# A 31-tap convolution shared by four engines: the shares, the place of the sums, and the last tiles by token halves

## The chip, the cores and the metric

The kernel runs on one core of a Trainium2 chip. The metric is the device time of one execution in microseconds (us). Before the change the median of three runs is 1353.84 us (1353.11 to 1364.42).

## The reference, cut to what matters

A program of two transformer-like blocks of two layers each, on 256 tokens of width 1024, all in fp32. The change is in one layer of the second block, the convolution layer. It is fed with a normalised `h` (256 tokens x 1024 features):

```python
def conformer_conv(h, w_pw1, b_pw1, w_dw, b_dw, ln_g, ln_b, w_pw2, b_pw2):
    a, gate = jnp.split(h @ w_pw1 + b_pw1, 2, axis=-1)
    u = a * jax.nn.sigmoid(gate)
    dw = lax.conv_general_dilated(           # each feature by itself, 31 taps back in time
        u, w_dw[:, None, :], window_strides=(1,), padding=((CONV_WIDTH_2 - 1, 0),),
        dimension_numbers=('NWC', 'WIO', 'NWC'), feature_group_count=D_MODEL) + b_dw
    d32 = dw.astype(jnp.float32)
    mu = jnp.mean(d32, axis=-1, keepdims=True)
    var = jnp.mean(jnp.square(d32 - mu), axis=-1, keepdims=True)
    z = (d32 - mu) * lax.rsqrt(var + EPS) * ln_g + ln_b
    z = jax.nn.silu(z).astype(h.dtype)
    return z @ w_pw2 + b_pw2
```

The mean and the variance go over all 1024 features of a token, so no token can be normalised before the last feature tile of that token is summed.

## The kernel before, in words

Every engine runs its own program (`pe_program` TensorE, `act_program` ScalarE, `dve_program` VectorE, `pool_program` GpSimd, `sp_program` the DMA queue). The order in each is written by hand. They meet only at named semaphore values (`sig`, `at`).

**Weights.** 200 chunks of up to 1 MB (`PLAN`) come through one DMA queue into three buffers `raw`. For each chunk ScalarE writes a rounded copy `whi` (`hi(n)`), VectorE the rest `wlo = raw - whi` (`lo(n)`), and TensorE multiplies in three passes, high x high, high x low, low x high (`mm3`). `hi(n)` waits until TensorE has done chunk n-3, and the DMA of chunk n until `lo(n-3)` is done.

**The convolution layer** has features on the partitions and tokens along the free axis: eight feature tiles of 128 x 256. `stationary` makes two 128 x 256 products of `w_pw1` from one chunk with 48 matmuls; eight chunks in all. Before the change a chunk holds two tiles of `a` or two of the gate, so tiles are ready in pairs, after each second chunk. ScalarE makes the sigmoid, VectorE `u` (a tile of `up`, signal `up{ft}`). The 31 taps of a tile are shared out: tap 0 with the bias is ScalarE's (`tap0`), the last `ON_PE[ft]` taps are matmuls with a diagonal matrix that holds the 128 weights of the tap (line 953), and the rest are VectorE's multiply-adds over 128 x 256 (line 1489) into `cv` in SBUF. ScalarE makes the diagonals too, one by one, in a ring of 12 (`diagonals`). VectorE adds TensorE's sum from PSUM (`add_taps`). GpSimd has no part in the taps.

**The norm** needs `cv` turned to tokens: `stats_of(t, c)` turns four tiles of token half t (line 405), VectorE takes the statistics (lines 2085, 2124), GpSimd the power -1/2 (lines 2243, 2171), VectorE normalises 128 x 512 pieces (line 1486), TensorE turns them back, ScalarE applies `silu` and rounds (`cz`, `chi`), VectorE makes the low part (`clo`). The output product with `w_pw2` (`rows_out`, 24 matmuls of 512 columns a chunk, 4 chunks) takes two feature tiles a chunk for all tokens at once, so it begins when the norm of both token halves is done.

The layers around it are SwiGLU layers (`ffn_stage`), bound by TensorE; the one before is number 2.

## Time and profile before

| What | Value |
|---|---|
| median of three runs | 1353.84 us |
| the profiled execution | 1352.12 us |
| its span in the trace | 1350.3 us |
| TensorE, VectorE, ScalarE, GpSimd busy | 96%, 68%, 53%, 4% of the span |
| mean granted TensorE clock | 0.989 |
| convolution layer, first matmul of `w_pw1` to the last of the taps | 1027.6 to 1120.3 us |
| from there to the first matmul of `w_pw2` | 1120.3 to 1129.8 us |
| from there to the turning of the next layer's input | 1129.8 to 1152.9 us |

The execution lasts 1.8 us longer than its span, for what lies around it. Times in the rows are microseconds from the span's start. A TensorE row's duration has latency in it that overlaps the next one, so matmuls are costed by the distance of their starts. The same holds for VectorE and ScalarE, to a smaller part.

### The profile page before, as it was taken

The page shows a single profiled execution, that of the slowest core. Times are in us where ns is not written, and L with a number is a line of the kernel's source. Part 1 is how long each engine was busy: PE and PEld are TensorE (multiplying, and loading weights), DVE is VectorE, ACT ScalarE, POOL GpSimd, SP SyncE. Part 2 cuts the span into 40 slices and gives each one's busy share as a digit, 9 for nine tenths or more (in the row PEclk, how much of TensorE's full clock was granted, in tenths as well). Part 3 has the DMA queues.
Part 4 walks back from the last instruction along what each step waited for, and adds up shares of the span by engine and source line. Part 5 has one row for each costly group of instructions (what it writes and reads, how often), then busy time and mean ns, then how long its engine had stood idle before and what let it go on. Part 6 is the DMA issues. An engine that isn't in the chain of part 4 may idle for free.

```text
span 1350.3 us, 17591 instructions
## 1 busy us (share of the span) xinstructions
PE 1291.1 (96%) x7034; PEld 1105.2 (82%) x7034; DVE 918.5 (68%) x1274; ACT 713.0 (53%) x1074; POOL 54.8 (4%) x80
## 2 busy tenths in 40 slices
PE   5999999999999878999999999999998998999997
PEld 5998778888888667888888877888888996888886
DVE  4967565766666676666667856766666896776665
ACT  5765444654445654554445544544446664554443
POOL 0000000100001400100000001000000000100000
PEclk9999999999999989999999999999999998999999
DMA  6453235455554411455555633555554321455551
GB/s 243 157 184 128 94 111 201 156 197 188 191 188 147 155 59 55 142 210 187 187 188 180 221 138 137 182 189 189 191 189 158 110 78 63 156 187 187 203 189 60
DMA packets 30785, 215.17 MB, mean 159 GB/s; under 512 B 3552, under 2 KB 3808, under 8 KB 5488
## 3 DMA queue, kind: packets, MB, share of 16 engines
q1 hardware_dynamic: 30704, 214.05, 45.0%
q8 instruction: 56, 0.92, 0.3%
q14 instruction: 25, 0.20, 0.0%
HBM read 212.99 MB, written 1.05 MB: 159 GB/s over the span
## 4 chain that ended last, share of the span: by engine, by line
PE 88%; DVE 5%; ACT 4%; POOL 1%; issue 1%; DMA 0%; SPq 0%; POOLq 0%; ACTq 0%; DVEq 0%
PE pb L428 23%; PE pb L399 15%; PE pb L401 14%; PE pb L400 14%; PE pb L430 11%; PE pb L953 3%; PE pb L405 2%; DVE wlo L1476 2%; ACT both L1020 1%; ACT whi L1016 1%; ACT arena L1020 1%; DVE arena L1480 1%; POOL st L2171 1%; PE pb L793 1%; DVE both L1489 1%
## 5 line engine op out<-in xcount | busy, mean ns | idle before, releaser
L1476 DVE TENSOR_TENSOR wlo<-raw,whi 128x2048 fp32r<-128x2048 f32 (+3 forms) x205 | 456.9, 2230 | 225.4 <-ACT whi L1016 225.2
L428 PE MATMUL pb<-both,whi 128*128 128x512 f32 x1344 | 477.0, 399 | 0.0
L1016 ACT ACTIVATE whi<-raw 128x2048 fp32r<-128x2048 f32 (+2 forms) x201 | 380.4, 1896 | 84.1 <-PE pb L401 81.6
L430 PE MATMUL pb<-both,wlo 128*128 128x256 f32 x1344 | 377.3, 281 | 0.0
L399 PE MATMUL pb<-whi,both 128*128 128x512 f32 (+1 forms) x754 | 298.2, 396 | 10.5 <-DVE both L1489 4.5
L428 PEld LDWEIGHTS pb<-both,whi 128*128 128x128 f32 x1344 | 252.5, 188 | 62.4
L401 PE MATMUL pb<-whi,both 128*128 128x512 f32 (+1 forms) x754 | 293.7, 390 | 0.0
L400 PE MATMUL pb<-wlo,both 128*128 128x512 f32 (+1 forms) x754 | 293.3, 389 | 0.0
L430 PEld LDWEIGHTS pb<-both,wlo 128*128 128x128 f32 x1344 | 253.8, 189 | 1.5
L1020 ACT ACTIVATE arena<-pb 128x256 f32<-128x256 f32 (+1 forms) x248 | 102.8, 427 | 259.7 <-PE pb L430 164.6
L399 PEld LDWEIGHTS pb<-whi,both 128*128 128x128 f32 x754 | 142.4, 189 | 43.1 <-issue 6.7
L401 PEld LDWEIGHTS pb<-whi,both 128*128 128x128 f32 x754 | 142.3, 189 | 30.8
L400 PEld LDWEIGHTS pb<-wlo,both 128*128 128x128 f32 x754 | 142.6, 189 | 26.7
L1480 DVE TENSOR_TENSOR arena<-arena 128x512 f32<-128x512 f32 (+3 forms) x187 | 122.1, 658 | 14.8 <-ACT arena L1020 3.8
L1480 DVE TENSOR_TENSOR arena<-arena,pb 128x256 f32<-128x256 f32 (+1 forms) x189 | 75.4, 423 | 53.2 <-ACT arena L1020 48.8
L399 PE MATMUL pb<-both,whi 128*128 128x256 f32 (+1 forms) x296 | 86.2, 291 | 3.5 <-DVE wlo L1476 2.4
L400 PE MATMUL pb<-both,whi 128*128 128x256 f32 (+1 forms) x296 | 84.4, 285 | 0.0
L401 PE MATMUL pb<-both,wlo 128*128 128x256 f32 (+1 forms) x296 | 84.3, 285 | 0.0
L1020 ACT ACTIVATE arena<-arena 128x512 f32<-128x512 f32 (+5 forms) x75 | 47.1, 632 | 68.4 <-DVE arena L1480 60.7
L1489 DVE SCALAR_TENSOR_TENSOR arena<-arena,cols 128x256 f32<-128x256 f32 x170 | 70.6, 480 | 6.0 <-ACT arena L1020 5.2
L405 PE MATMUL pb<-c,arena 128*128 128x128 f32 (+1 forms) x286 | 43.1, 296 | 22.1 <-ACT arena L1020 14.3
L1020 ACT ACTIVATE both<-arena 128x256 fp32r<-128x256 f32 x96 | 35.4, 412 | 52.8 <-DVE arena L1480 52.5
(121 smaller groups left out, 989.0 us busy)
## 6 DMA issues: line engine op xcount, KB each, us to landing
raw<-d_ws SPq DMA_DIRECT2D x196, 1024.0 KB, 4.9
raw<-d_ws SPq DMA_DIRECT2D x3, 768.0 KB, 4.3
arena<-d_c SPq DMA_DIRECT2D x1, 1060.0 KB, 4.9
xt<-d_x SPq DMA_DIRECT2D x2, 512.0 KB, 4.1
arena<-d_rows SPq DMA_DIRECT2D x2, 512.0 KB, 5.0
out<-arena SPq DMA_DIRECT2D x2, 512.0 KB, 2.6
raw<-d_ws SPq DMA_DIRECT2D x1, 640.0 KB, 3.8
c<-d_c SPq DMA_DIRECT2D x1, 385.0 KB, 5.0
```

Source lines behind the costliest of these rows:

```text
L399: e.matmul(out, lh, rh, start=start, stop=False)
L400: e.matmul(out, lh, rl, start=False, stop=False)
L401: return e.matmul(out, ll, rh, start=False, stop=stop)
L405: return e.transpose(out, a, ident[0:k, 0:k])
L428: e.matmul(b[:, :], wh[:, k, fs], both[:, k, :], start=k == 0, stop=k == 7, skip_group_check=True)
L430: m = e.matmul(b[:, 256:512], wl[:, k, fs], ahi[:, k, :], start=False, stop=k == 7, skip_group_check=True)
L953: m = e.matmul(b[:, 0:256], T.diag[:, tap[0] % NG, :], T.up[:, ft, w:w + 256], start=w == 31 - ON_PE[ft], stop=w == 30)
L1016: e.activation(whi[:, n % NH, 0:width(n)], raw[:, n % NR, 0:width(n)], ACT.Copy).then_inc(*sig("act.hi", f"hi{n}"))
L1020: e.activation(out, a, func, **kw).then_inc(*sig(key, *([name] if name else [])))
L1476: e.tensor_tensor(wlo[:, n % NH, a:b], raw[:, n % NR, a:b], f32(whi[:, n % NH, a:b]), ALU.subtract).then_inc(*sig("dve.lo", f"lo{n}"))
L1480: e.tensor_tensor(out, a, b, op).then_inc(*sig(key, *names))
L1489: e.scalar_tensor_tensor(out=out, in0=a, scalar=s, in1=b, op0=op0, op1=op1).then_inc(*sig(key, *names))
```

## The change

- **Shares of the taps.** TensorE has 79 taps in place of 106 (7, 8, 8, 8, 8, 9, 13, 18 by tile), VectorE 106 in place of 134, GpSimd sums 55 (7 or 8 a tile, 3 in the last). ScalarE makes GpSimd's products (`products`), in a ring of 12; the first one of a tile starts the sum `part`. GpSimd adds the others, 47 additions, and then `part` onto `cv` (`join`), once more a tile.
- **VectorE's sums lie in PSUM** (`acc`, banks 5 to 7). The last tap writes `cv` in SBUF. It works on two tiles in turn: the rest of one and the first `FIRST` taps of the next.
- **The diagonals are loaded**, 5 MB in five DMAs during SwiGLU layer 2, in place of being made by ScalarE.
- **Gates beside features.** The columns of `w_pw1` are interleaved, so that each chunk gives one tile's `a` and its gate, and a tile is ready with every chunk.
- **The last tiles, the norm and the output by token halves.** TensorE's taps of tiles 6 and 7 are done for tokens 0 to 127 first, and the norm of these goes on while the taps of the others are multiplied. `out_part` makes the first two chunks of the output for one token half at a time. GpSimd's sum of tile 7 goes in by a matmul with the identity.
- In all four SwiGLU layers ScalarE's last `hi` stands ahead of a wait for VectorE, not behind it.

```diff
 
-ON_PE = (12, 12, 12, 12, 12, 12, 17, 17)
-NG = 12
+ON_PE = (7, 8, 8, 8, 8, 9, 13, 18)
+ON_POOL = (7, 8, 7, 8, 7, 8, 7, 3)
+ON_DVE = tuple(30 - a - b for a, b in zip(ON_PE, ON_POOL))
+FIRST = (10, 7, 7, 7, 7, 7, 6, 15)
+DIAG0 = tuple(sum(ON_PE[:i]) for i in range(8))
+NX = 12
+AHEAD = 1
...
         self.mv = room(4)
-        self.diag = room(128 * NG, NG)
+        self.part = room(256 * 3, 3)
+        self.prod = room(256 * NX, NX)
...
                     sp_load(e, "pos", ret.pi, d_pos)
+                for i in range(len(DIAG_LOADS)):
+                    if n == CHUNK["gate2", 3 + i]:
+                        if i == 0:
+                            e.wait_ge(*at("x5.11"))
...
+                def taps(ft, name, spot, tokens, mid=None, then=None):
+
+                    b = claim(name, spot)
                     e.wait_ge(*at(f"up{ft}"))
...
-                    b = claim(f"ln{t}{c}")
+                    for i in range(ON_PE[ft]):
+                        n, w = DIAG0[ft] + i, 31 - ON_PE[ft] + i
+                        if i == mid:
+                            then()
+                        if i == 0 or n % 16 == 0:
+                            e.wait_ge(*at(f"in.diag{n // 16}"))
+                        m = e.matmul(b[:, 0:tokens.stop - tokens.start], T.diag[:, n, :],
+                                     T.up[:, ft, w + tokens.start:w + tokens.stop], start=i == 0, stop=w == 30 and ft < 7)
+                    if ft < 7:
+                        m.then_inc(*sig(key, f"{name}.m"))
+                    else:
+                        e.wait_ge(*at("sum7"))
+                        m = e.matmul(b[:, 0:128], ident, T.part[:, 1, tokens], start=False, stop=True)
+                        m.then_inc(*sig(key, f"{name}.m"))
...
+                for p in range(8):
+                    stationary(key, CHUNK["pw1", p], claim(f"p1.{p}", p % 3), f"p1m{p}", 6 if p == 0 else None)
+                    if 1 <= p <= 6:
+                        taps(p - 1, f"tp{p - 1}", 3 + (p - 1) % 2, slice(0, 256))
+                for ft in (5, 6, 7):
+                    ring.take(f"acc{ft}", 5 + ft % 3)
+                taps(6, "tp6.0", 3, slice(0, 128))
+                stats_of(0, 0, 2)
+                stats_of(1, 0, 0)
+                taps(7, "tp7.0", 1, slice(0, 128))
+                taps(6, "tp6.1", 7, slice(128, 256), 8, lambda: stats_of(0, 1, 5))
+                taps(7, "tp7.1", 4, slice(128, 256), 10, lambda: turn(0, 0, 3))
+                turn(0, 1, 2)
+                stats_of(1, 1, 7)
+                b0 = [claim(f"out6.0{c}", 4 + c) for c in range(2)]
+                out_part(0, 0, b0)
+                out_part(0, 1, b0, lambda: turn(1, 0, 1))
+                turn(1, 1, 0)
+                b1 = [claim(f"out6.1{c}", 6 + c) for c in range(2)]
+                out_part(1, 0, b1)
+                out_part(1, 1, b1)
+                for j in (2, 3):
...
                         e.wait_ge(*at(f"f{f}.h{j}"))
                         if j >= 2:
                             e.wait_ge(*at(f"done{CHUNK[f'down{f}', j - 2]}"))
                         for i in range(2):
                             run(key, f"f{f}.hhi{j}.{i}", ahi[:, 8 + (2 * j + i) % 4, :],
                                 ffn.hh[:, j % 2, 256 * i:256 * i + 256], ACT.Copy)
-                    if j == 10:
-                        hi(CHUNK[f"down{f}", 9] + 2)
                 if f > 1:
                     hi(CHUNK[f"down{f}", 10] + 2)
                     for c in range(2):
...
+                def products(ft, a, b):
+
+                    for i in range(a, min(b, ON_POOL[ft])):
+                        w = 1 + ON_DVE[ft] + i
+                        if i == 0:
...
+                        if made[0] >= NX:
+                            e.wait_ge(*at(f"summed{made[0] - NX}"))
+                        run(key, f"prod{made[0]}", T.prod[:, made[0] % NX, :], T.up[:, ft, w:w + 256], ACT.Copy,
+                            scale=col("w_dw", 8 * w + ft))
+                        made[0] += 1
+
+                def gate(ft):
+                    e.wait_ge(*at(f"p1m{ft}"))
+                    if ft >= 2:
+                        e.wait_ge(*at(f"up{ft - 2}"))
+                    run(key, f"sg{ft}", T.sg[:, ft % 2, :], bank(f"p1.{ft}")[:, 256:512], ACT.Sigmoid,
+                        bias=col("b_pw1", 8 + ft))
+
+                def first_tap(ft):
+                    e.wait_ge(*at(f"up{ft}"))
+                    e.wait_ge(*at(f"acc{ft - 3}.gone" if ft >= 3 else "sq6.11"))
+                    run(key, f"tap0.{ft}", bank(f"acc{ft}")[:, 0:256], T.up[:, ft, 0:256], ACT.Identity,
+                        scale=col("w_dw", ft), bias=col("b_dw", ft))
+
+                for p in range(8):
+                    if p:
+                        gate(p - 1)
+                    hi(CHUNK["pw1", p] + 2)
+                    if p:
+                        first_tap(p - 1)
+                        products(p - 1, 0, 4)
+                        if p == 7:
+                            gate(7)
+                        products(p - 1, 4, 31)
+                first_tap(7)
+                products(7, 0, 31)
+                run(key, None, T.sg[:, 0, 0:1], T.sg[:, 0, 0:1], ACT.Silu)
+                hi(CHUNK["pw2", 2])
...
+                def tap(ft, w, a=0, b=256):
+
+                    name, end = f"dwt{ft}" + (f".{a // 128}" if ft == 7 else ""), w == ON_DVE[ft]
+                    acc = bank(f"acc{ft}")[:, a:b]
+                    e.wait_ge(*at(f"tap0.{ft}" if w == 1 else name))
+                    stt(key, [name] + ([f"acc{ft}.gone"] if end and b == 256 else []), T.cv[:, ft, a:b] if end else acc,
+                        T.up[:, ft, w + a:w + b], col("w_dw", 8 * w + ft), acc, ALU.mult, ALU.add)
+
+                def taps(p, a, b):
+
+                    for i in range(a, b):
+                        w = 1 + FIRST[p - 1] + i
+                        if p and w <= ON_DVE[p - 1]:
+                            tap(p - 1, w)
+                        if i < min(FIRST[p], ON_DVE[p]):
+                            tap(p, 1 + i, 0, 128 if p == 7 else 256)
+
+                def gated(ft):
+                    e.wait_ge(*at(f"sg{ft}"))
+                    stt(key, [f"up{ft}", f"p1.{ft}.gone"], T.up[:, ft, 30:286], bank(f"p1.{ft}")[:, 0:256], col("b_pw1", ft),
+                        T.sg[:, ft % 2, :], ALU.add, ALU.mult)
+
+                def add_taps(ft, name, a=0, b=256):
+                    e.wait_ge(*at(f"{name}.m"))
+                    e.wait_ge(*at(f"dwt{ft}" + (f".{a // 128}" if ft == 7 else "")))
+                    tt(key, [("dx" if ON_POOL[ft] and ft < 7 else "dw") + name[2:], f"{name}.gone"], T.cv[:, ft, a:b], T.cv[:, ft, a:b],
+                       bank(name)[:, 0:b - a], ALU.add)
...
+                for p in range(8):
+                    if p:
+                        gated(p - 1)
+                        taps(p - 1, 0, AHEAD)
+                    lo(CHUNK["pw1", p] + 2)
+                    if p:
+                        taps(p - 1, AHEAD, 2 if p == 7 else 30)
+                    if p == 7:
+                        gated(7)
+                        taps(6, 2, 30)
+                    if p >= 2:
+                        add_taps(p - 2, f"tp{p - 2}")
+                taps(7, 0, 30)
+                add_taps(6, "tp6.0", 0, 128)
+                add_taps(7, "tp7.0", 0, 128)
+                stats_of(0, 0)
+                stats_of(1, 0)
+                for w in range(1, 2):
+                    tap(7, w, 128, 256)
+                stats_of(0, 1)
+                aggregate(0)
+                for w in range(2, 5):
+                    tap(7, w, 128, 256)
+                normal(0, 0)
+                normal(0, 1)
+                for w in range(5, ON_DVE[7] + 1):
...
             rstd_x("pool.conf", 6)
+            made = 0
+
+            def join(ft, name, a, b):
+
+                e.wait_ge(*at(f"dx{name}"))
+                tt("pool.conf", [f"dw{name}", f"part.gone{ft}"], conf.cv[:, ft, a:b], conf.cv[:, ft, a:b],
+                   conf.part[:, ft % 3, a:b], ALU.add)
+
+            for ft in range(8):
+                acc = conf.part[:, ft % 3, :]
+                for i in range(1, ON_POOL[ft]):
+                    if i == 1:
+                        e.wait_ge(*at(f"part{ft}"))
+                    else:
+                        own()
+                    e.wait_ge(*at(f"prod{made}"))
+                    tt("pool.conf", [f"summed{made}", f"sum{ft}"], acc, acc, conf.prod[:, made % NX, :], ALU.add)
+                    made += 1
+                if ft and ft < 7 and ON_POOL[ft - 1]:
+                    own()
+                    join(ft - 1, f"{ft - 1}", 0, 256)
             for t in range(2):
+                own()
+                join(6, f"6.{t}", 128 * t, 128 * t + 128)
```

On **TensorE**, behind the last `stationary` product of the kernel before, line 953 is a tap (two instructions in the trace) and line 405 a transpose:

```order
L953 MATMUL pb<-arena 128x256 x12
L405 MATMUL pb<-c,arena 128x128 x8
L953 MATMUL pb<-arena 128x256 x34
L405 MATMUL pb<-c,arena 128x128 x16
L399 MATMUL pb<-whi,both 128x512
```

The same place in the changed kernel, where line 971 is a tap, 977 the identity matmul, 417 a transpose and 411 the first output matmul:

```order
L971 MATMUL pb<-arena 128x128 x13
L417 MATMUL pb<-c,arena 128x128 x8
L971 MATMUL pb<-arena 128x128 x18
L977 MATMUL pb<-arena,c 128x128
L971 MATMUL pb<-arena 128x128 x8
L417 MATMUL pb<-c,arena 128x128 x4
L971 MATMUL pb<-arena 128x128 x15
L417 MATMUL pb<-c,arena 128x128 x4
L971 MATMUL pb<-arena 128x128 x8
L977 MATMUL pb<-arena,c 128x128
L417 MATMUL pb<-c,arena 128x128 x8
L411 MATMUL pb<-whi,both 128x512
```

The 12 and 34 taps of 256 tokens are now 13 and 18 for each half, and statistics and turned pieces of the first half stand between taps of the second.

On **VectorE**, one pair of tiles of the kernel before (line 1476 is `lo`, 1489 makes `u` or a tap, 1480 adds TensorE's sum):

```order
L1476 TENSOR_TENSOR wlo<-raw,whi 128x2048
L1480 TENSOR_TENSOR arena<-arena,pb 128x256 x2
L1489 SCALAR_TENSOR_TENSOR arena<-arena,cols 128x256 x22
L1476 TENSOR_TENSOR wlo<-raw,whi 128x2048
L1489 SCALAR_TENSOR_TENSOR arena<-pb,cols,arena 128x256 x2
L1489 SCALAR_TENSOR_TENSOR arena<-arena,cols 128x256 x14
```

One tile of the changed kernel (1542 makes `u` or a tap, 1529 is `lo`, 1533 adds):

```order
L1542 SCALAR_TENSOR_TENSOR arena<-pb,cols,arena 128x256
L1542 SCALAR_TENSOR_TENSOR pb<-arena,cols,pb 128x256 x2
L1529 TENSOR_TENSOR wlo<-raw,whi 128x2048
L1542 SCALAR_TENSOR_TENSOR pb<-arena,cols,pb 128x256 x12
L1542 SCALAR_TENSOR_TENSOR arena<-arena,cols,pb 128x256
L1533 TENSOR_TENSOR arena<-arena,pb 128x256
```

The taps read one tensor from SBUF and the sum from PSUM, where both lay in SBUF; each tile makes its round with one chunk.

On **GpSimd**, behind the power of the layer's first norm, nothing stood but the powers of the second one. Now:

```order
L2242 TENSOR_TENSOR arena<-arena 128x256 x53
L2242 TENSOR_TENSOR arena<-arena 128x128
L2337 TENSOR_SCALAR arena<-arena 128x1
L2242 TENSOR_TENSOR arena<-arena,c 128x1
L2242 TENSOR_TENSOR arena<-arena 128x128
```

The powers (2337 and 2242 on 128x1) stand behind 47 additions of products and six whole and one half `join`.

## Rows read from the trace of the kernel before

**Rows 1.** The page: busy time, share of the span, instructions of each engine.
```profile
PE 1291.1 (96%) x7034; PEld 1105.2 (82%) x7034; DVE 918.5 (68%) x1274; ACT 713.0 (53%) x1074; POOL 54.8 (4%) x80
PE 88%; DVE 5%; ACT 4%; POOL 1%; issue 1%; DMA 0%; SPq 0%; POOLq 0%; ACTq 0%; DVEq 0%
```

**Rows 2.** Stretches: length, busy time and count of each engine, clock, DMA.
```profile
1027.60:1120.30 92.70, 92.70 (x604) 86.97 (x605) 80.63 (x166) 60.19 (x137) 0.00 (x0) 1.00 0.26 92
1120.30:1129.80 9.50, 3.40 (x19) 2.50 (x17) 5.58 (x10) 1.56 (x4) 1.59 (x4) 0.81 0.00 1
1129.80:1153.30 23.50, 23.50 (x103) 19.34 (x104) 13.75 (x15) 12.61 (x20) 0.00 (x0) 0.93 0.34 115
```

**Rows 3.** The chain of waits in the layer: start, us, what.
```profile
1045.25 5.18 PE pb L953 x24
...
1056.19 5.18 PE pb L953 x24
...
1105.97 14.70 PE pb L953 x68
1120.69 0.43 DVE arena L1480
...
1129.79 0.77 PE pb L399
...
1130.98 0.43 PE pb L401
...
1133.58 0.23 PE pb L399
...
1152.93 0.45 PE pb L405 x4
```

**Rows 4.** Timeline of TensorE: start, us, line, operation, shape, count.
```profile
129.20 1.95 PE L601 MATMUL pb<-arena 128*128 128x128 f32 x16
...
1104.93 1.04 PE L405 MATMUL pb<-c,arena 128*128 128x128 f32 x8
```

**Rows 5.** Timeline of VectorE.
```profile
48.75 2.97 DVE L1489 SCALAR_TENSOR_TENSOR arena<-arena,cols 128x256 f32<-128x256 f32 x6 [0.32 <-ACT arena L1020]
...
94.17 1.12 DVE L1486 TENSOR_SCALAR arena<-pb,arena 128x128 f32<-128x128 f32 x4
...
1050.08 2.29 DVE L1476 TENSOR_TENSOR wlo<-raw,whi 128x2048 fp32r<-128x2048 f32 x1
1052.28 5.62 DVE L1489 SCALAR_TENSOR_TENSOR arena<-arena,cols 128x256 f32<-128x256 f32 x14
...
1108.72 10.38 DVE L1489 SCALAR_TENSOR_TENSOR arena<-arena,cols 128x256 f32<-128x256 f32 x26
```

**Rows 6.** Groups by shape, 1010 to 1170 us: busy us, mean ns, idle before.
```profile
L1480 DVE TENSOR_TENSOR arena<-arena,pb 128x256 f32<-128x256 f32 x12 | 4.6, 415 | 1.3 <-PE pb L953 1.3
...
L1020 ACT ACTIVATE arena<-arena,cols 128x256 f32<-128x256 f32 x8 | 4.4, 593 | 4.3 <-DVE arena L1489 4.3
...
L1480 DVE TENSOR_TENSOR both<-arena,both 128x256 fp32r<-128x256 f32 x10 | 4.2, 425 | 8.8 <-ACT both L1020 8.8
```

**Rows 7.** Timelines of VectorE and GpSimd around one `lo`.
```profile
1161.37 2.29 DVE L1476 TENSOR_TENSOR wlo<-raw,whi 128x2048 fp32r<-128x2048 f32 x1 [0.21 <-ACT whi L1016]
...
1161.45 2.62 POOL L2171 TENSOR_TENSOR st<-st,c 128x1 f32<-128x1 f32 x1
...
1164.53 0.55 POOL L2171 TENSOR_TENSOR st<-st,c 128x1 f32<-128x1 f32 x1
```

**Rows 8.** GpSimd's line 2171: min, median, max ns; six 128x32, six 128x512.
```profile
L2171 POOL TENSOR_TENSOR arena<-arena x12: 249/1290/3397, 448.5 to 473.4; 128x32 f32<-128x32 f32 x6, 128x512 f32<-128x512 f32 x6
```

**Rows 9.** SwiGLU layer 2: waits (total us, times, longest) and the stretch.
```profile
ACT whi L1016 <- PE pb L401: 15.0, 8, 1.9
...
860.00:1015.00 155.00, 155.00 (x811) 131.94 (x810) 102.65 (x116) 76.83 (x94) 0.00 (x0) 1.00 0.54 190
```

**Rows 10.** Timeline of VectorE at the end of SwiGLU layer 2.
```profile
1014.75 4.49 DVE L1476 TENSOR_TENSOR wlo<-raw,whi 128x2048 fp32r<-128x2048 f32 x2 [1.35 <-ACT whi L1016]
```

More of the change, by code:

```diff
@@ L93 @@
 STAGES = ("ssd", "ffn0", "mla", "ffn1", "ret", "ffn2", "conf", "ffn3", "end")
-LOADS = ("x0", "x1", "c0", "cols", "w2", "c1", "c2", "pw", "pos", "rows", "fg")
+DIAG_LOADS = tuple(f"diag{i}" for i in range(5))
+LOADS = DIAG_LOADS + ("x0", "x1", "c0", "cols", "w2", "c1", "c2", "pw", "pos", "rows", "fg")
 class Tally:
@@ L989, in conf_stage, with turn @@
-                ring.over = (0, 1, 2, 3)
-                turn(0)
-                for j in range(4):
-                    if j < 3:
-                        turn(j + 1)
-                    rows_out(key, 6, CHUNK["pw2", j], bs, (2 * j, 2 * j + 1), (f"clo{2 * j}", f"clo{2 * j + 1}"),
-                             j == 0, j == 3, (lambda: turn_half("pe.ffn3", 7, 0)) if j == 3 else None)
+                def turn(t, c, spot):
+                    b = claim(f"ct{t}{c}", spot)
+                    e.wait_ge(*at(f"dn{t}{c}"))
+                    for i in range(4):
+                        m = tr(b[:, 128 * i:128 * i + 128], T.dn[:, t, 512 * c + 128 * i:512 * c + 128 * i + 128])
+                    m.then_inc(*sig(key, f"ctm{t}{c}"))
@@ new lines, in out_part @@
+                def out_part(t, j, bs, mid=None):
+                    wh, wl = weights(CHUNK["pw2", j])
+                    for c in range(2):
+                        if mid and c:
+                            mid()
+                        for k in range(2):
+                            e.wait_ge(*at(f"clo{2 * j + k}.{t}"))
+                            m = mm3(bs[c][:, :], ahi[:, 2 * j + k, 128 * t:128 * t + 128],
+                                    alo[:, 2 * j + k, 128 * t:128 * t + 128], wh[:, k, half(c)], wl[:, k, half(c)],
+                                    j == 0 and k == 0, False)
+                    m.then_inc(*sig(key, *([f"done{CHUNK['pw2', j]}"] if t else [])))
@@ L1439, in turn @@
-                def turn(j):
-                    e.wait_ge(*at(f"ctm{j}"))
-                    for i in range(2):
-                        ft = 2 * j + i
-                        run(key, f"cz{ft}", T.cv[:, ft, :], bank(f"ct{j}")[:, 256 * i:256 * i + 256], ACT.Silu,
-                            scale=col("ln_g", ft), bias=col("ln_b", ft))
-                        own()
-                        run(key, f"chi{ft}", ahi[:, ft, :], T.cv[:, ft, :], ACT.Copy)
-                    tally.value[f"ct{j}.gone"] = at(f"cz{2 * j + 1}")
+                made = [0]
@@ L1449, in conf_stage @@
                 turn(0)
-                for j in range(3):
-                    turn(j + 1)
-                    hi(CHUNK["pw2", j] + 2)
+                turn(1)
+                hi(CHUNK["pw2", 3])
+                hi(CHUNK["pw2", 3] + 1)
             ssd_stage()
@@ L2121, in conf_stage, with aggregate @@
[L2121 to L2122 removed]
+                def aggregate(t):
                     own()
                     e.bn_aggr(T.mv[:, 2 * t:2 * t + 2], T.bst[:, 12 * t:12 * t + 12]).then_inc(*sig(key, f"cmv{t}"))
[L2125 to L2129 removed]
@@ new lines, in conf_stage @@
+                add_taps(6, "tp6.1", 128, 256)
+                add_taps(7, "tp7.1", 128, 256)
+                losses(0, range(0, 2))
+                stats_of(1, 1)
+                aggregate(1)
+                losses(0, range(2, 4))
+                normal(1, 0)
+                losses(0, range(4, 8))
+                normal(1, 1)
+                losses(1, range(3))
+                lo(CHUNK["pw2", 2])
+                losses(1, range(3, 8))
+                e.wait_ge(*at("in.rows"))
+                for t in range(2):
+                    tt(key, [], xt[:, t, :], xt[:, t, :], T.rows, ALU.add)
```

178 lines of the change are left out of this document (51 added, 127 removed).

## The prediction

> **What bounds the kernel now.** First the page: TensorE is busy for 96% of the span and holds 88% of the chain that ended last [rows 1]. The reader should see that a saving elsewhere is worth nothing unless TensorE waits for it. Then the stretches of the convolution layer [rows 2]: from 1027.6 to 1120.3 TensorE is busy for all of 92.7 us; from 1120.3 to 1129.8 it does 3.4 us of work and the granted clock is 0.81; then it is busy again, but at 0.93. The chain of waits [rows 3] gives the parts:
> - 12 taps start at 1045.25, last 5.18 and come again at 1056.19, so the 48 matmuls of a chunk take 10.94 - 5.18 = 5.76 us, and a tap 5.18/12 = 0.432. The last 34 taps say the same: 14.70/34 = 0.432. The stretch is 8 x 5.76 + 106 x 0.432 + 0.9 for eight transposes = 92.8 us. It is TensorE's own work and nothing else.
> - Then the norm stands open, 9.5 us from the last tap to the first output matmul (1129.79).
> - Behind it an output matmul takes 0.43 us, from 1133.1 on 0.23: after the pause TensorE is at the lower level of its clock, 1.2 GHz, then at 2.4. 90 output matmuls lie between 1129.79 and 1152.93, with 0.9 for eight transposes. At 0.2275 each that would be 21.4 us; it took 23.1, so the low clock costs 1.8.
>
> So the layer lasts 1152.93 - 1027.6 = 125.3 us. VectorE is busy for 80.6 of the first 92.7 us and ScalarE for 60.2 [rows 2]; these two are what limits how much can be moved off TensorE.
>
> **The change, part by part.**
>
> *TensorE.* Tiles 0 to 5 have 48 taps: 20.8 us. Tiles 6 and 7 have 31, each in two halves of 128 tokens. No tap of 128 tokens is in the trace; the nearest is line 601, eight products of 128x128 in 16 instructions that take (1.95 - 0.28)/15 = 0.112 each [rows 4] (0.28 is what one lasts), so 0.223 a product. Two halves cost 0.446 against 0.432 for a whole tap, and 62 halves 13.8 us; splitting costs 0.4 us in all. With eight chunks (46.1), two identity matmuls (0.4), 32 transposes, 0.45 for four [rows 3] (3.6), and 90 output matmuls (20.5) TensorE's own work to the same point is 105.2 us, against 114.0 before (125.3 less the 9.5 and the 1.8). The diagonals' making is off ScalarE; on TensorE that saves nothing.
>
> *VectorE.* A tap costs 10.38/26 = 0.40 where two tiles are taken in turn, and 0.50 where each waits for the one before ((2.97 - 0.48)/5) [rows 5]. Each tile's round is `lo` 2.20 (1050.08 to 1052.28), `u` 0.40, 13 or 14 taps 5.4, TensorE's sum 0.37: 8.4 us. I add 0.3 for the wait between `u` and the first tap of the tile, since ScalarE makes tap 0 in PSUM in between (0.59 at most [rows 6], against one other tap that covers 0.40), and 0.4 for GpSimd (below): 9.1. TensorE's round is 5.76 + 8 x 0.432 = 9.2. So they run almost even. Followed tile by tile from the first `u` at 1034.4, VectorE is through the first half of tile 7 at about 1104.5 (7 `lo` 15.4, 8 `u` 3.2, 97 taps 38.8 and 0.9 for the nine that stand alone, 9 half taps at (1.12 - 0.29)/3 = 0.28 [rows 5], in turn with others, 2.7, sums 2.8, waits for first taps 3.4, GpSimd 2.8). TensorE is there at 1027.6 + 46.1 + 20.8 + 13 x 0.223 + 0.9 + 19 x 0.223 = 1102.5. TensorE does 8 taps of the second half meanwhile (1.8 us) and then waits some 1 us for the last sums of the first.
>
> *The taps' sums in PSUM.* No VectorE row writes PSUM. An addition with an operand in PSUM takes 415 ns, one with all in SBUF 425 [rows 6], so I take the same 0.40. The bounds are 0.40 and 0.50, the distance at which taps follow each other singly. The Trainium skill (VectorE: DVE Perf Modes, The TRN2 errata) gives VectorE a fixed 120 cycles with a PSUM source against 58 from SBUF, which would add 0.065 us a tap, or 6.9 over 106, if it held; the two rows here don't show it. As a result of its own it is the first rival.
>
> *GpSimd.* Its additions of 32 and 512 elements take 0.249 and 1.290 us (least and median [rows 8]; the six of each shape stand below and above). On the line between them 256 elements take 0.74; with 0.08 for the wait between two, 0.81. Up to the sum of tile 7 it has 47 additions and six joins: 43 us. While VectorE runs a `lo`, it stands: an operation of 0.55 us took 2.62 when it was issued 0.08 after the start of one [rows 7]. Seven `lo` lie in its way: 7 x 2.2 = 15.4. So its round is 7.7 x 0.81 + 2.2 = 8.4, under 9.2, and from the first product at about 1037 it needs to 1095.8; as each tile's sum begins only with ScalarE's first product, I see it at 1102, just in time for tile 7. Ends: 0.25 and 1.29 an addition. The same row is why a `lo` may also wait for GpSimd, up to 0.74. The Trainium skill (SBUF, Who interferes with whom) calls it an exclusive lock of a pair of ports that VectorE takes with two inputs in SBUF; by that rule a tap with its sum in PSUM does not take it, and the row agrees for `lo`. No row here shows a tap beside GpSimd, in either form.
>
> *ScalarE.* Its round is `hi` 1.9, gate, tap 0 and 7 or 8 products at 0.59 or less [rows 6]: 7.5, hidden under 9.2. `hi` stands ahead of the products, so a late GpSimd does not hold the weights back until the ring of 12 is full.
>
> *The diagonals' loads.* 5 x 1 MB during SwiGLU layer 2, where the DMA engines are busy for 0.54 of the time and TensorE is never idle [rows 9]. ScalarE's `hi` waits there for TensorE alone, never for data, so the chunks come early. A chunk's 5.6 us of matmuls hold 3.0 us of transfer and 2.6 free; a load of 3.0 comes with every third chunk, into 7.8 free: 0. If the cover were gone, 5 x 3 = 15 us.
>
> *Norm and output.* The last half sums of tokens 0 to 127 are turned at about 1105.5. Statistics 0.65, aggregate 0.25, GpSimd 0.9 and two pieces of 0.7 take 3.5 to 4.2 us; TensorE has 15 half taps (3.3), and then turns the pieces and does 8 more (1.8). Second half: its last sum at about 1112.0, a `join` of 0.5, transposes to 1112.9. The output of the first token half begins there, 24 matmuls or 5.5 us, and the second norm (4 us) is inside it. The second half's 24 and the last 48 follow without a gap; both `lo` for them end 1 to 2 us early. The turning of the next input, at 1152.93 before, comes at 1112.9 + 0.9 + 90 x 0.2275 = 1134.3. The waits in this are about 1 us at the sums of the first half and 0.4 at the second join, so 105.2 + 1.4 = 106.6 from 1027.6 on, the same place. The 1.8 us of low clock go too, as no pause is over 1.5 us.
>
> *The moved `hi`.* At the end of SwiGLU layer 2, VectorE's two `lo` start at 1014.75 and end at 1019.2, after `hi` [rows 10]; with the first 1.4 us earlier the second starts 0.4 earlier, as it waits for TensorE. Gain 0.4 there, 0 in the other three, whose end is set by TensorE.
>
> **The sum.** 1152.93 - 1134.3 = 18.6, and 0.4: 19.0 us less. The profiled execution of 1352.1 would be 1333.1; the median of the runs is 1.7 higher, and gives 1334.8. Forecast 1335 us, 0.986 of before.
>
> **The rivals.**
> 1. *VectorE becomes the bound, since a sum in PSUM costs more.* At 0.50 a tap its round is 10.5 against 9.2. VectorE already ends 2 us behind TensorE, so some 97 x 0.1 = 9.7 us go onto the path: 1344.5. For it: VectorE was at 87% of this stretch. Against it: the 415 and 425 ns.
> 2. *GpSimd becomes the bound.* At 1.0 an addition with its wait, in place of 0.81, 53 x 0.19 = 10 us; 2 to 3 hide in its slack, 1343. For it: its round has only 0.8 to spare, and each `lo` blocks it. It would show as TensorE or VectorE waiting for line 2242.
> 3. *Taps and GpSimd's additions exclude each other*, as `lo` and GpSimd do [rows 7], even with the sum in PSUM. Then the 70 us of VectorE and the 43 of GpSimd come one after the other, and the first half is complete at 1034.4 + 113 = 1147 in place of 1105: 1335 + 42 = 1377, slower. It decides from the point where more than 19 of the 43 us are not beside the taps. The same ending has a smaller form: half of them blocked, 1356.
> 4. *The norm is not covered*: the second half's taps run out, TensorE pauses twice for 2 us more and comes back at the low clock, as in [rows 3], for 1.8: 1341.
>
> **How the numbers follow.** Forecast 0.67 (1331 to 1339), rivals 1 and 2 0.11 and 0.08, rival 3 0.05, rival 4 0.09. Lowest: no waits and no GpSimd delay, 2 us less, with TensorE alone setting the pace from 1331 on, and 1 for spread: 1330. The range 1330 to 1345 leaves out rival 3 and the upper parts of 1 and 2. About 1% (13.5 us) is what a measurement of this kernel can tell from no change. Faster by over 1%, under 1340.3: the forecast and a third of the others' chance, 0.75; within 1% 0.20; slower 0.05.
>
> **What would show it.** TensorE busy without a gap up to about 1094; tap pitch 0.432 and half tap 0.223; taps of VectorE at 0.40 with `pb` as output; GpSimd's 128x256 at 0.74, and longer only beside `lo`; first output matmul near 1113 in place of 1129.8, at 0.23. The forecast is wrong if a VectorE tap takes 0.5, if GpSimd's rows grow beside taps, or if TensorE waits for the weights in any chunk.

## The result, and the profile after

The changed kernel takes 1331.4 us (median of 4 runs, 1330.8 to 1333.6) against 1356.3 for the kernel before (4 runs, 1353.1 to 1364.4, the three of the forecast and one more): a ratio of 0.984, 95% interval 0.980 to 0.987. Forecast were 1335, range 1330 to 1345. The profiled execution took 1331.6, its span 1329.8. In the lines below `pb` is PSUM and `arena` SBUF.

The page, which answers to [rows 1]:

```profile
PE 1278.7 (96%) x7046; PEld 1098.0 (83%) x7046; DVE 911.4 (69%) x1265; ACT 704.0 (53%) x1040; POOL 105.7 (8%) x135
...
PE 89%; DVE 4%; ACT 4%; POOL 1%; issue 1%; DMA 0%; SPq 0%; POOLq 0%; ACTq 0%; DVEq 0%
```

TensorE is as busy as before; its stream is 12.4 us shorter, and GpSimd has 51 us of new work. The layer in stretches, against [rows 2]; behind the length stand the busy time and count of TensorE, its weight loads, VectorE, ScalarE and GpSimd, then the granted clock, the DMA share and GB/s:

```profile
1025.20:1094.00 68.80, 68.80 (x483) 66.26 (x484) 59.52 (x111) 44.01 (x77) 45.65 (x47) 0.97 0.33 115
1094.00:1104.20 10.20, 10.20 (x93) 10.09 (x93) 9.60 (x27) 6.56 (x11) 4.81 (x7) 1.00 0.15 63
1104.20:1111.30 7.10, 7.08 (x62) 6.72 (x61) 6.58 (x18) 2.70 (x10) 1.25 (x3) 1.00 0.00 1
1111.30:1132.70 21.40, 21.40 (x100) 17.64 (x100) 15.74 (x25) 11.79 (x30) 0.92 (x2) 1.00 0.41 145
```

The reader should see the second number beside the first in each row: TensorE is busy for all of the layer, and the stretch of 9.5 us with 3.4 of work is gone. The chain of waits, against [rows 3]:

```profile
1084.24 3.89 PE pb L971 x18
...
1093.88 2.90 PE pb L971 x26
...
1104.21 3.35 PE pb L971 x30
1107.58 0.63 PE pb L417 x4
...
1111.26 0.27 PE pb L411
...
1113.62 0.23 PE pb L412
...
1132.68 0.45 PE pb L417 x4
```

Nine taps of 256 tokens (18 instructions) take 3.89, 0.432 each; 13 of 128 take 2.90, 0.223 each. The first output matmul starts at 1111.26, 18.5 us sooner than before, and runs at 0.23 from the start. The next input is turned at 1132.68, 20.25 us sooner.

Where the 20.25 come from, by places that both traces have: 17.8 in the layer (from its first matmul at 1025.19 to 1132.68 are 107.5 us, 125.3 before), 0.5 in SwiGLU layer 2 ahead of it, and 1.9 earlier, of which 1.5 lie in the first layer, where no instruction was changed: from 19 to 26 us the granted clock was 0.76 in the trace before and 1.00 in this one. That part differs from one execution to the next and is not the change's.

The other engines, timelines of VectorE and, in the second fence, of GpSimd around one `lo`, against [rows 5] and [rows 7]:

```profile
1060.52 0.48 DVE L1542 SCALAR_TENSOR_TENSOR pb<-arena,cols,pb 128x256 f32<-128x256 f32 x1
1061.24 0.49 DVE L1542 SCALAR_TENSOR_TENSOR pb<-arena,cols,pb 128x256 f32<-128x256 f32 x1 [0.24 <-ACT pb L1055]
1061.64 2.28 DVE L1529 TENSOR_TENSOR wlo<-raw,whi 128x2048 fp32r<-128x2048 f32 x1
1063.84 4.79 DVE L1542 SCALAR_TENSOR_TENSOR pb<-arena,cols,pb 128x256 f32<-128x256 f32 x12
```
```profile
1060.35 0.75 POOL L2242 TENSOR_TENSOR arena<-arena 128x256 f32<-128x256 f32 x1 [0.53 <-DVE arena L1533]
1062.18 7.19 POOL L2242 TENSOR_TENSOR arena<-arena 128x256 f32<-128x256 f32 x7 [1.08 <-ACT arena L1055]
```

Twelve taps with their sum in PSUM take 4.79, so 0.40 each, while GpSimd adds beside them: seven additions from 1062.18 to 1069.37, through a `lo`. An addition alone lasts 0.74. VectorE was even ahead at the last chunk, where it stood for 2.29 us until the next tile's gate was there:

```profile
1094.42 0.48 DVE L1542 SCALAR_TENSOR_TENSOR arena<-pb,cols,arena 128x256 f32<-128x256 f32 x1 [2.29 <-ACT arena L1055]
```

The groups from 1005 to 1150, against [rows 6, 8] (busy us, mean ns, idle before):

```profile
L2242 POOL TENSOR_TENSOR arena<-arena 128x256 f32<-128x256 f32 x53 | 50.0, 944 | 28.9 <-ACT arena L1055 22.9 <-DVE arena L1533 2.9
...
L1542 DVE SCALAR_TENSOR_TENSOR pb<-arena,cols,pb 128x256 f32<-128x256 f32 x90 | 38.8, 485 | 3.5 <-ACT pb L1055 3.2
...
L1529 DVE TENSOR_TENSOR wlo<-raw,whi 128x2048 fp32r<-128x2048 f32 x16 | 36.5, 2288 | 7.1 <-ACT whi L1051 7.1
...
L1055 ACT ACTIVATE arena<-arena,cols 128x256 f32<-128x256 f32 x55 | 22.9, 496 | 0.0
```

GpSimd's 53 additions would be 39.2 us at 0.74; the 10.8 above that I put down to time under a `lo`, in which the additions stand. The `lo` itself lasts 2.29, as before.

### The profile page after: what moved, and what is told of

It reads as the page before. It is cut to its first block, busy times and chain, and to the rows that moved or that the text cites. A ratio compares the mean times of both kernels' runs of the same rounds, so it can differ in the third digit from the quotient of the medians.

```text
span 1329.8 us, 17700 instructions
## 1 busy us (share of the span) xinstructions
PE 1278.7 (96%) x7046; PEld 1098.0 (83%) x7046; DVE 911.4 (69%) x1265; ACT 704.0 (53%) x1040; POOL 105.7 (8%) x135
## 4 chain that ended last, share of the span: by engine, by line
PE 89%; DVE 4%; ACT 4%; POOL 1%; issue 1%; DMA 0%; SPq 0%; POOLq 0%; ACTq 0%; DVEq 0%
PE pb L440 23%; PE pb L411 15%; PE pb L413 15%; PE pb L412 15%; PE pb L442 12%; PE pb L971 3%; PE pb L417 2%; DVE wlo L1529 1%; ACT both L1055 1%; ACT whi L1051 1%; ACT arena L1055 1%; POOL st L2242 1%; PE pb L805 1%; DVE arena L1533 1%; DVE both L1542 1%
## 5 line engine op out<-in xcount | busy, mean ns | idle before, releaser
L1533 DVE TENSOR_TENSOR arena<-arena,pb 128x256 f32<-128x256 f32 (+2 forms) x191 | 75.9, 421 | 51.7 <-ACT arena L1055 48.1
L2250 POOL TENSOR_SCALAR st<-st 128x1 f32<-128x1 f32 (+2 forms) x26 | 9.4, 363 | 1111.9 <-DVE st L1533 917.8
L1055 ACT ACTIVATE arena<-arena 128x512 f32<-128x512 f32 (+6 forms) x76 | 47.3, 626 | 68.4 <-DVE arena L1533 60.8
L2242 POOL TENSOR_TENSOR arena<-arena 128x256 f32<-128x256 f32 (+3 forms) x67 | 65.5, 982 | 46.9 <-ACT arena L1055 22.9
L1055 ACT ACTIVATE both<-arena 128x256 fp32r<-128x256 f32 (+1 forms) x104 | 37.0, 396 | 47.1 <-DVE arena L1533 47.1
```

What stands on the lines that cost most here:

```text
L1055: e.activation(out, a, func, **kw).then_inc(*sig(key, *([name] if name else [])))
L1533: e.tensor_tensor(out, a, b, op).then_inc(*sig(key, *names))
L2242: e.tensor_tensor(out, a, b, op).then_inc(*sig(key, *names))
```

## The experiments

Each is the changed kernel with one edit. Whole times of one kernel scatter by up to 14 us (its granted clock between 0.981 and 0.994), so the layer's own length is read beside them: from its first matmul to the turning of the next input. A repeat of the changed kernel gives the measure for that.

> The changed kernel unaltered, beside the others of this set, as their reference. Expected 1331 us, and 107.0 to 107.5 us from the layer's first matmul to the turning of the next input. In the first profile 1.8 of the 107.5 lay in the first chunk of the layer, at a granted clock of 0.96. If that comes from what the change does there, it comes again; if it is the throttle's own doing, it may be gone, and the layer takes 105.7.

1334.5 us, ratio 0.987 [0.983, 0.991], and **105.85 us** for the layer (1030.94 to 1136.79). The granted clock around the layer's first matmul, in the first profile (it starts at 1025.19) and in this one (1030.94):

```profile
1023.00:1029.00 6.00, 5.44 (x26) 5.04 (x25) 3.98 (x9) 5.59 (x10) 0.00 (x0) 0.50 0.39 156
```
```profile
1023.40:1026.40 3.00, 0.00 (x0) 0.00 (x0) 2.17 (x7) 2.59 (x9) 1.21 (x3) 0.96 0.19 49
1027.00:1029.00 2.00, 2.00 (x11) 2.00 (x10) 0.49 (x1) 0.72 (x1) 0.03 (x1) 0.50 0.97 330
1029.90:1034.00 4.10, 3.20 (x27) 3.06 (x26) 3.23 (x9) 4.08 (x9) 0.00 (x0) 1.00 0.12 50
```

In both, TensorE stands for 3.4 us at a clock that is still high, and turns the layer's input for the most part at the low one (0.50, the level of 1.2 GHz). What differs is how long the low stretch lasts: about 3.4 us here, over before the first matmul, and 6.8 us in the first profile, to 1029.1. There it covers the first part of the layer's first chunk too, which takes 7.5 us from its first matmul to the next chunk's in place of 5.9. Of the eleven profiles with the change or parts of it two have the long stretch. The instructions are the same in both, and why it is long in some executions is not known. So 105.8 is the layer without it, and the measure below.

**1. The sums back in SBUF.** VectorE's running sums and ScalarE's tap 0 use `cv` in place of the PSUM bank.

```diff
-                    acc = bank(f"acc{ft}")[:, a:b]
+                    acc = T.cv[:, ft, a:b]
...
-                    run(key, f"tap0.{ft}", bank(f"acc{ft}")[:, 0:256], T.up[:, ft, 0:256], ACT.Identity,
+                    run(key, f"tap0.{ft}", T.cv[:, ft, :], T.up[:, ft, 0:256], ACT.Identity,
```

> VectorE's sums lie in SBUF again, all else as in the changed kernel. Theory 1, that place matters because VectorE and GpSimd exclude each other whenever VectorE reads two tensors in SBUF: GpSimd's 53 additions (43 us) no longer fit beside 106 taps, GpSimd's round grows from 8.2 us to about 14 us in place of 9.2, its 128x256 rows last 1 us and more in the mean over 0.944, and the kernel takes 25 to 45 us more than the changed one, 1355 to 1375 us. Theory 2, only the long subtractions exclude GpSimd and a tap of 0.4 us slips in between: within 3 us of 1331.4.

1353.6 us, ratio to before 1.000 [0.999, 1.002]; the layer takes 126.0. The whole gain hangs on this one edit. Its timeline of VectorE, of GpSimd, its groups, and what TensorE waited for (total, times, longest):

```profile
1060.32 7.75 DVE L1542 SCALAR_TENSOR_TENSOR arena<-arena,cols 128x256 f32<-128x256 f32 x12
```
```profile
1058.62 6.79 POOL L2242 TENSOR_TENSOR arena<-arena 128x256 f32<-128x256 f32 x6 [1.10 <-ACT arena L1055]
```
```profile
L1542 DVE SCALAR_TENSOR_TENSOR arena<-arena,cols 128x256 f32<-128x256 f32 x97 | 63.8, 711 | 2.4 <-ACT arena L1055 2.1
...
L2242 POOL TENSOR_TENSOR arena<-arena 128x256 f32<-128x256 f32 x53 | 52.9, 999 | 43.8 <-ACT arena L1055 23.0 <-DVE arena L1533 17.7
...
L971 PE MATMUL pb<-arena 128*128 128x256 f32 x96 | 25.4, 424 | 7.4 <-DVE arena L1542 7.4
```
```profile
PE pb L971 <- DVE arena L1542: 10.1, 6, 2.3
PE pb L977 <- POOL arena L2242: 3.3, 1, 3.3
PE pb L417 <- POOL arena L2242: 1.7, 1, 1.7
```

Twelve taps take 7.75 in place of 4.79. A tap rises from 485 to 711 ns in the mean, 21.9 us over 97, while an addition of GpSimd rises from 944 to 999 only, 2.9 us over 53: it is VectorE that loses, 0.47 us for each of the 47 additions ahead of the last sum. The round of a tile goes from 9.0 to 12.1 us in the mean of six, and TensorE stands for 15.1 us, two thirds of it for line 1542. The granted clock, 0.96 from 1034 to 1080 and 0.95 from there to 1112, takes 3.4 more. My expectation had the loser wrong, GpSimd, and 1353.6 lies just below its 1355 to 1375.

The means hide how clean the split is. Single instructions, an addition with the tap beside it, a tap with no addition beside it, and an addition that met a `lo` (1058.11 to 1060.39):

```profile
1061.07 0.81 POOL L2242 TENSOR_TENSOR arena<-arena 128x256 f32<-128x256 f32 x1
```
```profile
1061.19 0.97 DVE L1542 SCALAR_TENSOR_TENSOR arena<-arena,cols 128x256 f32<-128x256 f32 x1
...
1067.59 0.47 DVE L1542 SCALAR_TENSOR_TENSOR arena<-arena,cols 128x256 f32<-128x256 f32 x1
```
```profile
1058.62 2.37 POOL L2242 TENSOR_TENSOR arena<-arena 128x256 f32<-128x256 f32 x1 [1.10 <-ACT arena L1055]
```

Of the 97 taps 50 lie beside an addition and last 0.83 to 0.97 us; 45 have none beside them and last 0.47 to 0.49, with a product of ScalarE beside them (10) or without; two meet only the edge of one. So ScalarE's products are not the cause. A tap and an addition together take 0.88 from one pair to the next, where additions in the changed kernel follow each other every 0.81: VectorE goes at GpSimd's pace. In these pairs the addition starts ahead of the tap, mostly by 0.13 us, and under a `lo` it starts behind it. In both it is the one that starts second that stands.

**2. The same without GpSimd's additions.** Sums in SBUF as in run 1, and the 45 additions of tiles 0 to 6 with their products left out (the output lacks those taps). One product a tile and the joins stay, a join waits for that product, and VectorE's and TensorE's shares stay as they are.

```diff
-ON_POOL = (7, 8, 7, 8, 7, 8, 7, 3)
-ON_DVE = tuple(30 - a - b for a, b in zip(ON_PE, ON_POOL))
+ON_DVE = tuple(30 - a - b for a, b in zip(ON_PE, (7, 8, 7, 8, 7, 8, 7, 3)))
+ON_POOL = (1, 1, 1, 1, 1, 1, 1, 3)
```

> VectorE's sums in SBUF as in the run with the sums in SBUF, and GpSimd's additions of 128x256 left out but for tile 7: 38 or so products and their additions are not computed, so the output lacks those taps; VectorE, TensorE and the joins are as in the changed kernel. Theory (with sums in SBUF a tap and an addition of GpSimd exclude each other, and nothing else is slow about SBUF): the taps are back at 0.40, VectorE's round at 9 us or less, the layer lasts 105 to 107 us as in the changed kernel. Rival (a tap with its sum in SBUF is slow by itself): the round stays at 11.5 and the layer at 126.

```profile
L1542 DVE SCALAR_TENSOR_TENSOR arena<-arena,cols 128x256 f32<-128x256 f32 x97 | 43.3, 501 | 2.4 <-ACT arena L1055 2.1
```
```profile
1056.19 4.83 DVE L1542 SCALAR_TENSOR_TENSOR arena<-arena,cols 128x256 f32<-128x256 f32 x12
```
```profile
1070.99 0.74 POOL L2242 TENSOR_TENSOR arena<-arena 128x256 f32<-128x256 f32 x1 [8.73 <-DVE arena L1533]
```
```profile
1071.13 0.88 DVE L1542 SCALAR_TENSOR_TENSOR arena<-arena,cols 128x256 f32<-128x256 f32 x1
```

Timeline and groups show the taps back at 0.40, and the layer at 107.4 (1027.77 to 1135.15), 1334.0 us in the one run. So the place of the sum is free by itself and costs only beside an addition of GpSimd. The last two rows show the rest: where one of the remaining joins lies beside a tap, that tap takes 0.88 again. Five taps do so, and one beside tile 7's additions takes 0.95. These six cost VectorE 2.5 us, and the 1.6 us of the layer over 105.8 are mostly a wait of TensorE of 1.4 us for the first half's last sum.

**3. The norm behind the taps.** The statistics of the first half stand behind all of the second half's taps.

```diff
-                taps(6, "tp6.1", 7, slice(128, 256), 8, lambda: stats_of(0, 1, 5))
-                taps(7, "tp7.1", 4, slice(128, 256), 10, lambda: turn(0, 0, 3))
+                taps(6, "tp6.1", 7, slice(128, 256))
+                taps(7, "tp7.1", 4, slice(128, 256))
+                stats_of(0, 1, 5)
+                turn(0, 0, 3)
```

> TensorE turns the sums and the normalised pieces of the first token half only after all taps of the second. Theory 1, the cover by taps is what removed most of the old pause: the chain of turning, statistics, power and normalising (about 3.9 us, from 1103.7 to 1107.6) and the turning back stand open, the first output matmul comes 4 to 6 us later, with some 1 us of low clock, so 1336 to 1338. Theory 2, the split output alone does it, since its second half has work anyway: under 1.5 us more.

1341.3 us, ratio 0.990 [0.985, 0.995]; the layer takes 113.2 (1031.68 to 1144.89), 7.4 over 105.8. Its chain and its window:

```profile
1113.84 0.45 PE pb L417 x4
1114.31 0.71 DVE arena L2158
...
1119.86 0.69 PE pb L417 x2
```
```profile
1112.00:1136.00 24.00, 19.65 (x93) 15.77 (x92) 16.08 (x38) 11.66 (x34) 2.28 (x5) 0.86 0.09 31
```

TensorE stands for 4.35 us in this window, at whose granted clock of 0.86 another 3.4 of the 24 us are lost. Covering the norm by half taps is worth 7.4 us of the gain. That is more than my expectation, which had 1 us for the clock; rival 4 had priced the loss at 6.

**4. Two more taps a tile on TensorE**, taken from GpSimd (14 in all, the two of tile 6 in halves, tile 7 as it was; a sixth load brings the diagonals).

```diff
-ON_PE = (7, 8, 8, 8, 8, 9, 13, 18)
-ON_POOL = (7, 8, 7, 8, 7, 8, 7, 3)
+ON_PE = (9, 10, 10, 10, 10, 11, 15, 18)
+ON_POOL = (5, 6, 5, 6, 5, 6, 5, 3)
```

> Two taps more on TensorE and two less on GpSimd in each of tiles 0 to 6; 93 diagonals, six loads. Theory 1, TensorE sets the pace of the whole layer: 12 x 0.432 for tiles 0 to 5 and 2 x 0.446 for tile 6 make 6.1 us more, 1337.5. Theory 2, VectorE or GpSimd set it: 0 to 3 us more, as GpSimd's relief pays for part.

1339.6 us, ratio 0.989 [0.986, 0.993]; the layer takes 111.45, 5.6 more. Twelve whole taps and four half ones are 12 x 0.432 + 4 x 0.223 = 6.1: the work added is paid nearly in full, so TensorE sets the pace of the changed kernel. The 0.5 are small waits that it had, spread over the transposes and half taps behind 1100: the distances there are longer in the repeat of the changed kernel (1.01 against 0.84 us for the last eight transposes ahead of the output) and count as busy time.

**5. The other way: six, three, and six with another order on GpSimd.** Taps of tiles 0 to 5 go from TensorE to VectorE, one a tile or in tiles 0, 2 and 4 only. In the third kernel GpSimd adds tile 7's products before it joins tile 5.

```diff
-ON_PE = (7, 8, 8, 8, 8, 9, 13, 18)
+ON_PE = (6, 7, 7, 7, 7, 8, 13, 18)
```
```diff
-ON_PE = (7, 8, 8, 8, 8, 9, 13, 18)
+ON_PE = (6, 8, 7, 8, 7, 9, 13, 18)
```
```diff
-ON_PE = (7, 8, 8, 8, 8, 9, 13, 18)
+ON_PE = (6, 7, 7, 7, 7, 8, 13, 18)
...
-                if ft and ft < 7 and ON_POOL[ft - 1]:
+                if ft and ft != 6 and ON_POOL[ft - 1]:
                     own()
-                    join(ft - 1, f"{ft - 1}", 0, 256)
+                    join(ft - 1 if ft < 7 else 5, f"{ft - 1 if ft < 7 else 5}", 0, 256)
```

> One tap of each of tiles 0 to 5 goes from TensorE to VectorE. Theory 1, TensorE is the bound and VectorE has the 2.3 us of slack that it showed at the last chunk: 6 x 0.432 = 2.6 us off TensorE, 6 x 0.40 = 2.4 on VectorE, so 1 to 2.5 us less, 1329 to 1330.5. Theory 2, VectorE is already the second bound within a tile: the same or up to 2 us more.

> Taps of tiles 0, 2 and 4 on TensorE are 6, 7 and 7 in place of 7, 8 and 8, VectorE has one more in each. Theory (TensorE sets the pace, VectorE and GpSimd have about 1 us of room in all): 3 x 0.432 = 1.3 us less for TensorE, of which the waits for the last sums of VectorE and for GpSimd's sum of tile 7 take some back: 1330.4 us, layer 0.7 us shorter. Rival (with six moved VectorE was the bound already, and the engines are even as they are): 0 or up to 1 us slower.

> The kernel with six taps more on VectorE, and GpSimd adds tile 7's products before it joins tile 5. There TensorE waited 2.1 us for GpSimd's sum of tile 7, which stood behind that join, and the granted clock fell to 0.95 for it; the layer took 107.0. Theory (GpSimd's order made that wait): the sum is ready 1.4 us earlier, TensorE waits 0.5 to 1.0 us for VectorE's last sums of the first half in its place, the layer lasts 104 to 105 us. Rival (VectorE is late by as much): the wait stays, with line 1542 or 1533 as releaser, 106 to 107.

| taps moved | time us | ratio to before | layer us | work less | result |
|---|---|---|---|---|---|
| 3 | 1331.4 | 0.984 [0.982, 0.986] | 104.7 | 1.3 | 1.1 less |
| 6 | 1334.2 | 0.987 [0.982, 0.991] | 107.0 | 2.6 | 1.2 more |
| 6, sum of tile 7 first | 1334.1 | 0.986 [0.983, 0.990] | 108.2, with 1.7 of the long low stretch: 106.5 | 2.6 | 0.7 more |

What TensorE waited for from 1030 to 1130 (total, times, longest), with six moved, and with the sum of tile 7 first:

```profile
PE pb L977 <- POOL arena L2242: 2.1, 1, 2.1
```
```profile
PE pb L417 <- POOL arena L2242: 2.0, 1, 2.0
PE pb L977 <- POOL arena L2242: 0.6, 1, 0.6
```

The granted clock behind that wait, with six moved:

```profile
1104.20:1107.40 3.20, 3.19 (x15) 3.19 (x16) 3.02 (x10) 0.00 (x0) 0.46 (x1) 0.50 0.00 0
```

With three moved TensorE stands for 0.15 us from 1034 to 1112, and the layer is shorter by nearly all of the work taken off. With six it waits 2.1 us and then runs at the low clock for 3.4 us, which costs 1.7: 2.1 and 1.7 less the 2.6 of work are the 1.2 more. With the third kernel the clock stays at 1.00 there; its waits of 2.6 take back the work, and the 0.7 are small waits as in run 4. The other order turned that wait into one for the first half's join, which stands behind VectorE's last sum: the rival of that run was right, VectorE is late by as much. So the room of VectorE and GpSimd was between three and six taps. The kernel with three moved has the shortest layer of all and the same time as the changed kernel; a microsecond is less than these whole times tell apart.

**6. The five loads at once.** All are issued ahead of one weight chunk.

```diff
-                    if n == CHUNK["gate2", 3 + i]:
+                    if n == CHUNK["gate2", 5]:
```

> The five loads of the diagonals are issued one behind the other, ahead of one weight chunk of SwiGLU layer 2, in place of one in every third chunk. 5 MB take 15 us at 3.0 a load. Theory of the prediction (a load is free only while it fits into the time that the weight chunks leave): the next chunk comes 15 us later than it would; the ring holds three chunks of raw weights, of which about two (11.5 us of matmuls) are still unused when a new one is ordered, so TensorE waits for 2 to 6 us in the stretch from 860 to 1012, with ScalarE's hi as releaser. Rival (the queues carry the loads side by side with the chunks, or the ring covers it all): 0, TensorE busy for all of the stretch.

1335.3 us, ratio 0.989 [0.984, 0.994]; the layer takes 105.8. The issues on the DMA queue, and two windows:

```profile
883.61 2.63 SPq L356 DMA_DIRECT2D arena<-d_diag  x5
890.94 21.54 SPq L386 DMA_DIRECT2D raw<-d_ws  x5
```
```profile
884.00:897.00 13.00, 13.00 (x69) 11.03 (x68) 8.33 (x10) 7.24 (x9) 0.00 (x0) 1.00 0.99 398
...
860.00:1012.00 152.00, 152.00 (x798) 129.48 (x797) 101.02 (x115) 75.38 (x92) 0.00 (x0) 1.00 0.62 227
```

My theory of a loss of 2 to 6 us fell. The DMA engines are full for 13 us (0.99, 398 GB/s, so 5.2 MB), and TensorE is busy for all of the 152 us, exactly as with the loads spread out. The cover is larger than the 2.6 free us a chunk that I had counted: ScalarE's `hi` goes on during the burst (886.68, 890.48 and 895.76), and in the 152 us it waits for TensorE only, 15.0 us in all as with the loads spread out, so the chunks already ordered last through it.

**7. The `hi` where it stood before.** It goes behind the copies of the hidden rows again, for each layer's last down chunk.

```diff
-                        hi(CHUNK[f"down{f}", j - 1] + 2 if j else CHUNK[f"gate{f}", 1] + 2)
+                        if j < 10:
+                            hi(CHUNK[f"down{f}", j - 1] + 2 if j else CHUNK[f"gate{f}", 1] + 2)
...
+                    if j == 10:
+                        hi(CHUNK[f"down{f}", 9] + 2)
```

> The hi of the last down chunk of each SwiGLU layer goes back to where it stood before, behind the copies of the hidden rows; all else as changed. Theory of the prediction: 0.4 us slower at the end of SwiGLU layer 2, nothing in the others, 1331.8 us in all. Rival (the measured 0.46 came from elsewhere, or the order matters in every layer): 0, or 4 x 0.4 = 1.6.

1333.4 us, ratio 0.987 [0.982, 0.992]; the layer takes 105.85. VectorE's two `lo` stand one behind the other again, as in [rows 10]:

```profile
1014.99 4.49 DVE wlo L1532 x2
```

The place to measure is the turning of the convolution layer's input, which waits for this end. From the turning of the second half of SwiGLU layer 2's input (834.45 us in the kernel before) to it are 189.3 us in this kernel and in the one before, against 188.8 to 189.1 in all ten with the early `hi`. So the early `hi` is worth 0.2 to 0.5 us there, of the size foretold. At the layer's first matmul this is no longer to be seen: 193.5 us here and 193.1 before, against 192.4 to 193.3 in the ten, as the turning itself takes 3.6 to 4.2 us by how much of it falls under the low clock.

## Why the prediction was right, step by step

- **TensorE's own work to the anchor**, forecast 105.2 and with waits 106.6 from the layer's first matmul: 105.85 where the first chunk runs at full clock, 107.5 in the first profile, whose long low stretch no term of the forecast had. Chunk, tap 0.432, half tap 0.223 and the 90 output matmuls came as put: from 1111.26 to 1132.68 are 21.4 us, of them 0.9 for the eight transposes, 0.228 each. Run 4 shows that this sum sets the pace.
- **The waits**, forecast 1.0 at the first half's last sums and 0.4 at the second join: 0.02 us of idle time in the window 1034 to 1112, in both profiles of the changed kernel, and the 0.65 over the own work are no one wait (0.5 of them vanish in run 4). This is the term that was too large. I had VectorE through the first half 2 us behind TensorE, with 0.4 a tile in it that `lo` would wait for GpSimd. `lo` lasts 2.29 as before, VectorE even stood for 2.29 us at the last chunk, and it was through 1.6 us behind TensorE (1103.3 against 1101.7), which the eight half taps between cover.
- **VectorE**, forecast 0.40 a tap and 9.1 a round: 4.79/12 = 0.40; rounds of 9.33 and 8.75 us (`u` at 1060.12, 1069.45 and 1078.20). The wait for tap 0 was 0.24, of 0.3 allowed. Rival 1 (0.50 a tap) fell. The Trainium skill (VectorE: DVE Perf Modes, The TRN2 errata) gives a larger fixed cost with a PSUM source, 0.065 us a tap by the estimate in the prediction. It is not seen: taps with the sum in PSUM last 472 to 491 ns, taps with all in SBUF and no addition beside them 468 to 487 (run 2), and both follow each other every 0.39 to 0.40 us.
- **GpSimd**, forecast 0.74 an addition, 2.2 for each of seven `lo`: 0.74, and 10.8 us under `lo` in place of 15.4; it also waits for products while a `lo` runs (1.08 us behind 1061.1, for one). In the repeated run its sum of tile 7, forecast "just in time", ended at 1104.81, 0.8 us before TensorE came to the identity matmul that needs it (1105.58). Rival 2 fell; in run 5, with 2.6 us less work on TensorE, this sum is late by 2.1 us behind a join that waits for VectorE, and by 0.6 without it.
- **Taps beside additions**, the step for which the trace before had no row. With the sum in PSUM they run side by side, as taken; with the sum in SBUF VectorE goes at GpSimd's pace, and the gain is 0. The only rows that bore on it were those of `lo`, and its price was guessed in rival 3 alone. Rival 3 named the right mechanism on the wrong side of its condition. That its smaller form, 1356, lies near the 1353.6 of run 1 is partly luck: it took half of GpSimd's 43 us as blocked, and what was lost are 0.47 us of VectorE for each of 47 additions. The rule of the Trainium skill (SBUF — State Buffer, Who interferes with whom), by which VectorE, outside its two-port modes, contends with GpSimd only with two inputs in SBUF, is borne out here by runs 1 and 2 for short taps and not only for `lo`.
- **ScalarE**, products at 0.59 or less: 0.496 in the mean, and TensorE waits for none.
- **The loads of the diagonals**, forecast 0: 0, and TensorE busy for 152.00 of 152.00 us. The 15 us "if the cover were gone" priced something that not even five loads at once bring about.
- **Norm and output**, forecast covered, first output matmul 85.3 us after the layer's first matmul: 86.1 with the slow first chunk in it, 84.3 without. Run 3 shows what the cover is worth, 7.4.
- **The moved `hi`**, forecast 0.4: 0.2 to 0.5 at the place where it acts, by run 7. How much of it reaches the layer's first matmul is not shown.
- **The total**, forecast 18.6 for the layer and 0.4 for the `hi`: the layer gave 19.5 at full clock and 17.8 in the first profile. The measured ratio gives 1.3 to 2.0%; forecast was 1.4%. The medians are 24.9 us apart, and the 5.9 us over the forecast are no term of it; I put them down to the scatter of whole times: two of the four runs before took 1358.7 and 1364.4 us, and in the later set the medians of the two kernels were 1352.4 and 1334.5. The chance of "faster by over 1%" was put at 0.75; 0.67 and a third of the rivals' 0.33 make 0.78.
